# Reordering the head of a two-layer diffusion step: x and the first projection chunk before the last modulation pair, smaller bias rows, a later bias table

## The reference, cut to what matters

```python
for l in range(2):
    mod = silu(c) @ w_ada[l] + b_ada[l]            # 6 rows of 1024: shift, scale, gate, twice
    h = rms_norm(x, norm_g[l, 0]) * (1 + sc_m) + sh_m
    q, k, v, u, vm, bg, cg, hx = split(h @ w_in[l])    # 1024 x 2816
    o_att = neighbourhood_attention(q, k, v, cache_k, cache_v, rpb[l])   # s = q k / 8 + bias from rpb
    y = concat(o_att, gated_mlp(u, vm), short_conv(bg, cg, hx)) @ w_out[l]
    x = x + gt_m * rms_norm(y, norm_g[l, 1])
    h = rms_norm(x, norm_g[l, 2]) * (1 + sc_f) + sh_f
    f = swiglu(h) if l == 0 else top2_of_8_experts(h)
    x = x + gt_f * rms_norm(f, norm_g[l, 3])
```

## Time and profile before

| | |
|---|---|
| median of 3 runs | 1600.64 us (1600.35 to 1601.16) |
| profiled execution, its own time | 1607.02 us |
| its span, first to last instruction | 1605.2 us |
| TensorE busy | 1526.6 us, 95% of the span |
| VectorE / ScalarE / GpSimd busy | 63% / 54% / 11% |
| chain that ended last | PE 88%, DVE 4%, DMA 3%, ACT 2% |
| weights moved | 398 MB on the queue of SP, 267 GB/s over the span for all |

### The profile page before, as it was taken

The page is one execution under the profiler, slowest core; times in us unless marked ns, Lnnn a source line. Parts: engine busy times, 40 slices in busy tenths (PEclk is TensorE's granted clock), DMA queues, the critical chain, the costliest instruction groups (busy, mean ns, idle before and its releaser), DMA issues.

```text
span 1605.2 us, 26359 instructions
## 1 busy us (share of the span) xinstructions
PE 1526.6 (95%) x11100; PEld 1240.8 (77%) x11100; DVE 1016.7 (63%) x935; ACT 865.0 (54%) x874; POOL 169.3 (11%) x175
## 2 busy tenths in 40 slices
PE   3989999999999999998999999999999989999993
PEld 3767777888888788787888888888888878777872
DVE  1425664333323554567988889888888966765665
ACT  1525543232222554546777777777777755554553
POOL 3120000000000310013002030300303010002001
PEclk8999999999999999999999999999999999999997
DMA  9994254777666573145999999999999988778882
GB/s 304 332 276 149 83 156 132 226 221 250 214 213 261 144 250 117 56 152 205 380 367 384 379 375 387 369 381 374 384 374 379 388 299 274 265 266 283 273 284 95
DMA packets 216658, 429.33 MB, mean 267 GB/s; under 512 B 23346, under 2 KB 64370, under 8 KB 215904
## 3 DMA queue, kind: packets, MB, share of 16 engines
q1 hardware_dynamic: 200448, 397.99, 71.1%
q0 software_dynamic: 14272, 22.66, 4.9%
q10 hardware_dynamic: 1808, 6.86, 1.1%
HBM read 422.65 MB, written 22.45 MB: 277 GB/s over the span
## 4 chain that ended last, share of the span: by engine, by line
PE 88%; DVE 4%; DMA 3%; ACT 2%; issue 1%; SPq 1%; ACTq 0%; POOL 0%; DVEq 0%; POOLq 0%
PE ps L1584 26%; PE ps L1586 25%; PE ps L1585 25%; PE ps L2087 3%; PE ps L1626 2%; DMA raw<-in_w_in_dram 2%; PE ps L2120 1%; PE ps L2054 1%; DMA raw<-in_w_ada_dram 1%; ACT whi L747 1%; DVE wlo L1078 1%; PE ps L1772 1%; DVE x L1176 1%; PE ps L1756 1%; PE ps L1741 1%
## 5 line engine op out<-in xcount | busy, mean ns | idle before, releaser
L1078 DVE TENSOR_TENSOR wlo<-raw,whi 128x2048 fp32r<-128x2048 f32 x327 | 745.8, 2290 | 343.0 <-ACT whi L747 249.7
L747 ACT ACTIVATE whi<-raw 128x2048 fp32r<-128x2048 f32 x327 | 626.4, 1918 | 470.1 <-PE ps L1586 233.0
L1584 PE MATMUL ps<-whi,xhi 128*128 128x512 f32 (+1 forms) x1352 | 536.6, 397 | 5.2 <-DVE xlo L1156 3.4
L1586 PE MATMUL ps<-whi,xlo 128*128 128x512 f32 (+1 forms) x1352 | 523.3, 387 | 0.0
L1585 PE MATMUL ps<-wlo,xhi 128*128 128x512 f32 (+1 forms) x1352 | 523.1, 387 | 0.0
L1584 PEld LDWEIGHTS ps<-whi,xhi 128*128 128x128 f32 x1352 | 255.0, 189 | 63.6 <-issue 9.7
L1586 PEld LDWEIGHTS ps<-whi,xlo 128*128 128x128 f32 x1352 | 254.8, 188 | 52.9
L1585 PEld LDWEIGHTS ps<-wlo,xhi 128*128 128x128 f32 x1352 | 255.2, 189 | 47.2
L1584 PE MATMUL ps<-whi,hhi 128*128 128x512 f32 x484 | 192.8, 398 | 0.0
L1586 PE MATMUL ps<-whi,hlo 128*128 128x512 f32 x484 | 188.9, 390 | 0.0
L1585 PE MATMUL ps<-wlo,hhi 128*128 128x512 f32 x484 | 188.6, 390 | 0.0
(11 more groups left out here) (231 smaller groups left out, 1054.6 us busy)
## 6 DMA issues: line engine op xcount, KB each, us to landing
raw<-in_w_moe_gu_dram SPq DMA_DIRECT2D x352, 512.0 KB, 5.7
raw<-in_w_moe_d_dram SPq DMA_DIRECT2D x176, 512.0 KB, 5.1
raw<-in_w_ada_dram SPq DMA_DIRECT2D x96, 512.0 KB, 6.2
raw<-in_w_in_dram SPq DMA_DIRECT2D x44, 512.0 KB, 5.2
raw<-in_w_ffn_gu_dram SPq DMA_DIRECT2D x44, 512.0 KB, 7.2
raw<-in_w_ffn_d_dram SPq DMA_DIRECT2D x22, 512.0 KB, 6.3
raw<-in_w_out_dram SPq DMA_DIRECT2D x16, 512.0 KB, 4.2
bias<-rpb_rows POOLq DMA_DIRECT2D x32, 96.0 KB, 6.4
```

Source lines behind the costliest of these rows:

```text
L747: act.activation(whi[m % SPL][:, :], raw[n % RING][:, :], ACT.Copy).then_inc(s_hi, 1)
L1078: dve.tensor_tensor(wlo[n % RING][:, :], raw[n % RING][:, :], whi[NTH[n] % SPL][:, :].bitcast(F32), ALU.subtract).then_inc(s_lo, 1)
L1584: pe.matmul(out, a_hi, w_hi, start=start, stop=False)
L1586: return pe.matmul(out, a_lo, w_hi, start=False, stop=stop)
```

## The change

In the stream, the first projection chunk moves two places forward: chunks 0 to 5 are ada, 6 is the first projection chunk, 7 and 8 are the last two ada chunks of the head. From chunk 9 on the stream is as before. Chunk 6 is still multiplied after chunks 7 and 8, so the count `s_pe` no longer goes up in the order of the stream; a function `done(n)` gives the count at which chunk n is done (9 for chunk 6, n for 7 and 8, n + 1 for all others), and the loads wait for that. x is loaded after four chunks.

The bias rows and norm rows are written to the partitions 0, 32, 64, 96 and 1, 33, 65, 97 alone: two transfers of four pieces of 512 bytes for a bias row, two of eight pieces for both halves of a norm row. The tiles are cleared once beforehand. The repeated rows get a tile of their own (`repeated`), and their write to memory is issued after the transposes of x. DVE's wait for that write goes away, and ACT waits for it before the first write to `pr`. ACT fetches its square-root table before x is there. In the head TensorE turns seven of the eight column blocks before block 3 of the modulation, with more filler matmuls (`warm`) in places, and results of the head's modulation blocks lie in columns 384 to 511 of their banks. The bias table is read back after position 5 rather than 3, and DVE adds the mask right ahead of unit 4's softmax.

```diff
-X_AFTER = 5
+X_AFTER = 4
...
     out = [("ada", 0, j) for j in range(2 * HEAD)]
+    out.insert(2 * HEAD - 2, ("win", 0, WIN_SEQ[0]))
     for l in range(DEPTH):
         for p, w in enumerate(WIN_SEQ):
-            out.append(("win", l, w))
+            if l or p:
+                out.append(("win", l, w))
...
+def done(n):
+
+    first = PLACE["win", 0, WIN_SEQ[0]]
+    return first + 3 if n == first else n if first < n <= first + 2 else n + 1
...
             def load(n):
                 if n >= RING:
-                    sp.wait_ge(s_pe, n - RING + 1)
+                    sp.wait_ge(s_pe, done(n - RING))
...
-                pool.dma_start(brow_of[:, i % 2, :],
-                               bass.AP(b_ada.tensor, b_ada[l, 512 * i:512 * i + 512].offset, [[P, 4], [0, 32], [1, P]])
-                               ).then_inc(s_brow[i % 2], 16)
+                for g in range(2):
+                    pool.dma_start(brow_of[g:P:32, i % 2, :],
+                                   b_ada[l, 512 * i:512 * i + 512].rearrange("(j n) -> j n", j=4)
+                                   ).then_inc(s_brow[i % 2], 16)
...
-            pool.wait_ge(s_rep, 1)
-            pool.dma_start(rpb_rows.rearrange("l r q j -> (l r) (q j)"),
-                           f[0:7 * NH * DEPTH, 0:2, :].rearrange("p t n -> p (t n)")).then_inc(s_rows, 16)
...
                     pool.wait_ge(s_tr, KT)
+                    pool.wait_ge(s_rep, 1)
+                    pool.dma_start(rpb_rows.rearrange("l r q j -> (l r) (q j)"),
+                                   repeated[0:7 * NH * DEPTH, :]).then_inc(s_rows, 16)
...
-                    pool.wait_ge(s_pe, PLACE["win", 0, WIN_SEQ[3]] + 1)
+                    pool.wait_ge(s_pe, PLACE["win", 0, WIN_SEQ[5]] + 1)
                     bias_rows(l)
...
                 if s == 0:
+                    act.wait_ge(s_const, N_CONST)
+                    fetch_roots()
                     act.wait_ge(s_x, 32)
-                    act.wait_ge(s_const, N_CONST)
...
             for i in range(HEAD):
                 ada(0, i)
-                if i == 2:
+                if i == HEAD - 3:
                     scaled(0, 0, 0)
+                if i == HEAD - 2:
+                    upto(PLACE["win", 0, WIN_SEQ[0]])
             mod_columns(0, 0)
-            upto(PLACE["win", 0, WIN_SEQ[0]])
...
                         for u in units_at(j, 0):
+                            if u == N_OWN and l == 0:
+                                masked_bias(l)
                             if u == N_OWN:
                                 dve.wait_ge(s_bias, l + 1)
...
-                    if p == (3 if l else 6):
+                    if p == 3 and l:
                         masked_bias(l)
...
+                    if i == HEAD - 1:
+                        for kt in range(4):
+                            turn_x(0, kt)
+                        ada_turn(0, HEAD - 2)
+                        for kt in range(4, KT - 1):
+                            turn_x(0, kt)
+                        warm(6, 4)
                     ada(0, i)
-                    if i:
+                    if 0 < i < HEAD - 1:
                         ada_turn(0, i - 1)
-                        if i < HEAD - 1:
-                            warm(6, 4)
-                for kt in range(5):
-                    turn_x(0, kt)
+                        warm(6, 4)
+                warm(3, 4)
                 ada_turn(0, HEAD - 1)
-                turn_x(0, 5)
-                pe.wait_ge(s_modr, HEAD)
-                turn_x(0, 6)
-                pe.wait_ge(s_modc, 1)
-                turn_x(0, 7)
+                warm(8, 4)
+                turn_x(0, KT - 1)
```

More of the change, by code:

```diff
@@ L410, in look, with ada_out @@
             return 1 if p <= 5 and l == 0 or p == 1 and l else 2
-        def ada_bank(l, i):
-            return 6 if (l, i) in ADA_IN_FFN else 5 + i % 2
+        def ada_out(l, i):
+            if l == 0 and i < HEAD:
+                return ps[:, 5 + i % 2, NT * P:NT * P + P]
+            return ps[:, 6 if (l, i) in ADA_IN_FFN else 5 + i % 2, 0:P]
         def ffn_src(gu, dn, j):
@@ L576, in norm_row @@
                     pool.wait_ge(s_modr, ADA_B * l + 6 * (j // 2))
[L577 to L579 removed]
+                for g in range(2):
+                    pool.dma_start(grow[g:P:32, :, :], norm_g[l, j].rearrange("(h j n) -> j h n", h=2, j=4)
+                                   ).then_inc(s_gb, 16)
+            chain(pool.memset(brow_of[:, :, :], 0.0))
+            chain(pool.memset(grow[:, :, :], 0.0))
             brow(0, 0)
@@ L1097, in ada @@
             def ada(l, i):
-                n = PLACE["ada", l, 2 * i + 1]
-                dve.wait_ge(s_pe, n + 1)
-                bank = ada_bank(l, i)
-                dve.wait_ge(s_brow[i % 2], 16 * (ADA_B // 2 * l + i // 2 + 1))
+                dve.wait_ge(s_pe, done(PLACE["ada", l, 2 * i + 1]))
+                dve.wait_ge(s_brow[i % 2], 32 * (ADA_B // 2 * l + i // 2 + 1))
                 mod, h = divmod(i, 2)
@@ L1111, in ada @@
                     gate = (gate_m if mod == 2 else gate_f)[:, h, :]
-                    chain(dve.tensor_tensor(gate, ps[:, bank, 0:P], row, ALU.add))
+                    chain(dve.tensor_tensor(gate, ada_out(l, i), row, ALU.add))
                     dve.tensor_tensor(gate, gate, grow[:, h, :], ALU.mult).then_inc(s_modr, 1)
@@ L1116, in ada @@
                         dve.wait_ge(s_colmm, turned(ADA_B) * l + turned(i - 2))
-                    dve.tensor_tensor(mrow[:, i % 2, :], ps[:, bank, 0:P], row, ALU.add).then_inc(s_modr, 1)
+                    dve.tensor_tensor(mrow[:, i % 2, :], ada_out(l, i), row, ALU.add).then_inc(s_modr, 1)
             def mod_columns(l, half):
```

17 lines of the change are left out of this document (7 added, 10 removed).

## The result

| | before | with the change |
|---|---|---|
| median (range) | 1600.64 us (1600.27 to 1601.16, 5 runs) | 1591.60 us (1588.32 to 1593.54, 5 runs) |
| ratio of the times, 95% interval | | 0.994 (0.9928 to 0.9951) |
| profiled execution, span | 1607.02, 1605.2 us | 1591.60, 1589.9 us |
| TensorE busy | 1526.6 us | 1527.8 us |

The kernel became 9 us faster, where 15.1 were forecast. The time lies in the range, but 6 us above the forecast value, so something was missing. Both kernels were run again: before 1601.38 us, changed 1590.13 us (ratio 0.9938, 0.9925 to 0.9951). So the medians put the gain at 9 to 11 us.

A forecast was written before the change was run, and what follows sets the result against it. TensorE was taken to be busy nearly everywhere but the first slice, so only its waits could be won: head 7.1, position 5 9.0, mask -1.0, together 15.1 us, from 1600.64 to 1585.5, range 1582 to 1593.

The forecast's parts named there:

- Term (a): Head: writing the 0.92 MB of repeated rows behind the loads lands the last ada chunk 2.4 us earlier.
- Term (b): Head: smaller bias and norm rows free the load queue by 3.1 us, between 1.1 by bytes and 3.8 as measured.
- First product at 42.3: Head: TensorE's first product comes at 42.3 us instead of 48.53, after the last ada chunk lands at 37.8.
- its statistics and 21 transposes are done while the last chunks fly: Head: work on x is hidden under the last loads; without that cover it would cost up to 3 us.
- The clock stays at 1.00 through the first projection chunk: Behind the first product: no slow-clock products, so the chunk takes 8.8 us instead of 10.4 and ends at 51.1.
- (c), chunk 14: Behind the first projection chunk: its held ring buffer delays later loads, a new TensorE wait of 0.7 us (0 to 3).
- The order of the chunks: Head: the projection chunk lands two chunks (5.4 us) earlier, at 32.4, split by 36.6, so its split leaves the chain.
- Position 5, 9.0 us: Without bias transfers the chunk lands 6.0 us after issue; 6.8 us of idle, 0.7 of transposes, 1.5 of last step gained.
- The mask, 1.0 us (0 to 2.5): Ahead of unit 4's softmax: result about 2 us later, against 0.7 slack and 0.8 won before; net cost 1.0 us.
- The rest of the program does the same work: Everything after the head, position 5 and the mask: no change in time counted.
- the one with a smaller head: Rival, 1589.5 us: rows cost only bytes, clock falls in the first chunk, or chunk 14 is 2 us later; chance 0.20.
- the one with a smaller position 5: Rival, 1592 us: chunk lands 3 us later, part of the clock is lost, mask costs 2.5; chance 0.12.

The follow-up runs named there:

- the kernel with all edits: Changed kernel with fewer fillers in the head, first projection chunk one place forward instead of two, mask in four pieces: 1585.38 us, ratio 0.9897.
- the last two kernels: Changed kernel with fewer fillers and mask in four pieces, first projection chunk one place forward (1585.38 us) or two (1588.28 us).

## Why the prediction was right where it was, and where it failed

The sign, the two places and most terms were right. What fell short were two terms of the sum, the wait for chunk 14 and the mask, and two that it set to nothing: TensorE's own queue in the head, and the rest of the program.

- **Term (a), repeated rows, 2.4 us**: right, 2.5 by the run with the early write. **Term (b), small rows, 3.1 us**: right, 3.3 to 3.6 for the six ahead of the projection chunk. Both together moved the last chunk from 43.28 to 36.86, 6.4 us for a forecast of 5.5, so the measured end of (b), 3.8, would have been the better choice. (The prediction counts seven such transfers issued before 43.28. The trace has eight, but the last, at 42.57, came too late to matter.)
- **First product at 42.3**: 43.81 in one execution, 42.29 in the other, and the second was on time by luck of the clock. The landing was even better than the 37.8 forecast: 36.9, as the run with fewer fillers shows. The step that failed is "its statistics and 21 transposes are done while the last chunks fly". They were to be hidden, and the prediction gave the price of that cover, up to 3 us, but never added up TensorE's own queue: turns, 12 fillers, 21 transposes and 12 fillers last 7.7 us from 30.76 on, most of it with the clock at 0.57, and end at 38.4, not 36.9. With the fillers cut the first product came at 41.18, 1.1 earlier than forecast.
- **The clock stays at 1.00 through the first projection chunk**: right, in all traces of the changed kernel. The chunk took 9.2 and 8.8 us (8.8 forecast). The clock was down ahead of it, which the prediction left out: in the first execution 0.51 in 18 to 24 us and 0.50 in 24 to 30, where TensorE was busy for 3.0 of 6 us; in the second 1.00 and 0.63. That is where the two executions part.
- **(c), chunk 14, 0.7 us**: the mechanism was right, the size 1.5 to 1.7. A wait for this chunk was one of the signs that the prediction named for being wrong. The chunk was counted to land 10.8 us after the end of the first projection chunk; it took 12.1 (52.97 to 65.05) and 12.2 in the second execution. TensorE came when it was expected, 15.1 us after that end.
- **The order of the chunks**: the prediction credited it with taking the split out of the chain. The run with the old order shows that it was worth nothing in the time: TensorE ended the head anyway, and the 1.3 us that the old order lost ahead of the first product came back at the third projection chunk.
- **Position 5, 9.0 us**: right, 9.2 and 9.3, with the chunk split from 106.29 on, 6.0 us after its issue began (100.31), and 0.37 of the 7.26 left.
- **The mask, 1.0 us (0 to 2.5)**: 1.7 in one execution, 3.2 in the other, above the bound. The sum behind it doesn't give 1.0: a result 2 us later less 0.7 of slack is 1.3, and 0.5 with the 0.8 taken off too. Counted from the end of position 5, the softmax of unit 4 began at 27.0 us instead of 24.7 and its result was there 2.3 later, which less the slack is 1.6. The step that failed is to set "0.8 won before" against it. TensorE did come 0.7 us earlier to this place (26.85 instead of 27.55), but there it waits for DVE, so this only made its wait longer, 2.40 us and not the 1 to 2 forecast. DVE was hardly early: free for the mask or the softmax at 23.7 instead of 24.0, not the 1 us counted. The other 1.5 us of the second execution are the clock: in 134 to 140 TensorE was busy for 3.7 us of 6, and the next 6 us had 0.72. The prediction put nothing on that.
- **"The rest of the program does the same work"**: true for the work, not for the time. At the gather the changed kernel was 12.1 us ahead; the medians differ by 9 to 11. See below.

Of the rivals, the one with a smaller head came nearest in mechanism (chunk 14 later, 1589.5; it came 1.3 later than counted, not 2), and the mask's bound was in the one with a smaller position 5 (1592), whose main part, a late landing, didn't happen. The bias table was never late.

## What to carry to other kernels

When a transfer is taken out of a chain, add up the queue of the engine that was waiting for it, at the clock that the trace shows there: fillers and moved work that looked hidden may now be what ends last. A large piece of moved work on a helper engine goes best in slices between the waits of the main engine: the mask cost TensorE a wait of 2.4 us in one piece of 3.35 us and none in four of 0.95. And when the engine that waits comes earlier while the one it waits for doesn't, nothing is won. Whether a reorder itself pays should be tried apart from the bytes that are removed with it: here the order of the chunks gave nothing that could be measured.

## What the runs showed of the hardware that was not expected

**The same wait is followed by the lower clock in some executions and not in others.** The wait of 2.40 us behind the mask left the clock at 1.00 in five of eight traces and was followed by 0.72 over 6 us in three, 1.5 us more. Both happened with one and the same kernel. The clock differs between executions in the head too (0.57 or 0.80 in 30 to 36 with the same instructions). What decides it, the runs don't show.

**The last experts vary from trace to trace.** TensorE sits idle for 1.3 to 2.3 us as expert 5 ends, in all 14 traces, on nothing that the profile shows. What comes after differs. Waits of TensorE behind 1290 us, in the profile before:

```profile
PE ps L2087 <- issue: 3.3, 8, 1.0
PE ps L2014 <- issue: 2.1, 1, 2.1
```

in its second execution:

```profile
PE ps L2014 <- issue: 1.6, 1, 1.6
```

and in the changed kernel:

```profile
PE ps L2103 <- issue: 1.7, 2, 1.4
PE ps L2030 <- issue: 1.3, 1, 1.3
```

In the changed kernel's second execution there is no such second stall, but the clock is down in the five us behind the end of expert 5:

```profile
1297.77:1302.77 5.00, 5.00 (x24) 3.73 (x26) 0.42 (x1) 1.85 (x1) 3.98 (x4) 0.66 0.81 274
```

Each trace but three has one of the two: a second stall (four traces) or a clock of 0.66 to 0.73 (seven). From the result of expert 5 to that of expert 6 they take 136.8 to 137.7 us (139.0 in the first execution before), and the three with neither (the second before, the run with fewer fillers alone, and the one with the early write) 135.1 to 135.8. So the second execution before had neither and the changed kernel one each time, which is 2 us and most of what it lost between the gather (12.4 and 12.9 us ahead of that execution) and the end (9.5 and 11.4). Why the one or the other comes, and whether the changed kernel meets it more often, the runs leave open: there are two traces of each. A like loss of 1.9 us stands behind the gather in the kernel with all edits (clock 0.91 over 723 to 743 in the last two kernels, 1.00 in all others): 571.3 us from the gather to the result of expert 5, against 569.2 to 569.9 in eight traces. Five more lie between, at or above that (570.4 to 572.8, the changed kernel's first execution at 570.5), four of them with no such clock. With the 2.6 us of expert 6 that is what the kernel with all edits lost of its lead: its span, 1584.6, is 14.8 below that of the second execution before.
